# Expert weights loaded four tiles at a time, in runs of 32 KB, in a two-block transformer kernel

## The reference, cut to what matters

```python
def moe_expert_choice(h, router_w, w_gate, w_up, w_down):
    B_, T, _ = h.shape
    cap = CAPACITY_FACTOR * T // N_EXPERTS          # 32
    aff = jax.nn.softmax((h @ router_w).astype(jnp.float32), axis=-1)
    gate, idx = lax.top_k(jnp.swapaxes(aff, 1, 2), cap)
    xs = h[bidx, idx]
    hid = jax.nn.silu(jnp.einsum('becd,edf->becf', xs, w_gate)) * jnp.einsum('becd,edf->becf', xs, w_up)
    ye = jnp.einsum('becf,efd->becd', hid, w_down) * gate[..., None].astype(h.dtype)
    return jnp.zeros_like(h).at[bidx, idx].add(ye)
```

## Time and profile before

| | before |
|---|---|
| runs, median (lowest to highest) | 1550.55 us (1549.97 to 1551.77), 3 runs |
| profiled execution | 1551.3 us |
| its span, first to last instruction | 1549.5 us |
| TensorE busy | 1207.3 us, 78% of the span |
| VectorE, ScalarE busy | 562.5 us, 423.9 us |
| TensorE's granted clock, mean | 0.89 |
| moved by DMA | 520.9 MB, 336 GB/s over the span |
| packets of the SP queue | 118496 |

### The profile page before, as it was taken

One profiled execution on the slowest core, in us unless ns is written; L12 is line 12 of the kernel. 1 busy time (PEld: TensorE's weight loads), 2 busy tenths in 40 slices (PEclk: granted clock), 3 DMA queues, 4 the chain that ended last, 5 costly groups with the idle time before them and its releaser, 6 DMA issues.

```text
span 1549.5 us, 18615 instructions
## 1 busy us (share of the span) xinstructions
PE 1207.3 (78%) x8122; PEld 730.7 (47%) x8122; DVE 562.5 (36%) x829; ACT 423.9 (27%) x553; POOL 29.9 (2%) x36
## 2 busy tenths in 40 slices
PE   4999999999656656656666656656666899999998
PEld 1878899943111212111111111211211589999997
DVE  3887776511101101101101101101101497777566
ACT  2865646232000000000000000000000454467545
POOL 0012000000000000000000000000000000000000
PEclk9999999999778878778867888878778999999999
DMA  9546859699999999999999999999999855555551
GB/s 364 207 156 229 301 209 337 223 403 429 426 428 428 428 428 427 428 428 426 428 428 427 427 428 428 427 427 429 428 427 428 327 164 163 163 183 184 184 186 55
DMA packets 118719, 520.90 MB, mean 336 GB/s; under 512 B 7264, under 2 KB 85088, under 8 KB 90736
## 3 DMA queue, kind: packets, MB, share of 16 engines
q1 hardware_dynamic: 118496, 519.64, 83.9%
q10 hardware_dynamic: 144, 0.09, 0.0%
HBM read 518.66 MB, written 1.05 MB: 335 GB/s over the span
## 4 chain that ended last, share of the span: by engine, by line
DMA 53%; PE 43%; DVE 2%; ACT 1%; SPq 1%; issue 0%; DVEq 0%
DMA pair<-in_wu 27%; PE B L1697 16%; DMA pair<-in_wd 12%; DMA pair<-in_wg 11%; PE B L1705 6%; PE B L2113 4%; PE B L1709 3%; DMA wslot<-in_w_in 2%; PE B L1824 2%; PE B L2147 1%; PE B L1675 1%; PE B L1812 1%; PE B L1827 1%; DMA wslot<-in_w_out 1%; DMA wslot<-in_ada_w 1%; PE B L2074 0%
## 5 line engine op out<-in xcount | busy, mean ns | idle before, releaser
L2113 PE MATMUL B<-pair,xs 128*32 128x512 f32 x2048 | 323.1, 758 | 193.0 <-DMA pair<-in_wu 121.5
L2113 PEld LDWEIGHTS B<-pair,xs 128*32 128x32 f32 x2048 | 63.2, 124 | 413.0 <-issue 180.1
L2147 PE MATMUL B<-pair,hidT 128*32 128x512 f32 x1008 | 167.9, 799 | 102.1 <-DMA pair<-in_wd 96.6
L1697 PE MATMUL B<-hnh,whj 128*128 128x256 f32 x488 | 138.1, 283 | 0.0
L1697 PE MATMUL B<-hnh,wslot_r 128*128 128x256 f32 x488 | 137.6, 282 | 0.0
L1697 PE MATMUL B<-hn_r,whj 128*128 128x256 f32 x488 | 137.1, 281 | 0.0
L2147 PEld LDWEIGHTS B<-pair,hidT 128*32 128x32 f32 x1008 | 32.3, 128 | 218.6 <-DMA pair<-in_wd 143.2
L955 DVE TENSOR_TENSOR wslot_r<-wslot,whj 128x2048 fp32r<-128x2048 f32 x52 | 118.9, 2289 | 31.3 <-ACT whj L509 31.3
L509 ACT ACTIVATE whj<-wslot 128x2048 fp32r<-128x2048 f32 x51 | 97.2, 1913 | 87.6 <-PE B L1697 82.0
L1289 DVE SCALAR_TENSOR_TENSOR x<-B,mod,x 128x256 f32<-128x256 f32 x128 | 56.0, 480 | 163.5 <-PE B L2092 163.3
L1320 DVE COPY ye<-B 128x512 f32<-128x512 f32 x15 | 10.4, 692 | 269.6 <-PE B L2147 269.6
(11 more groups left out here) (505 smaller groups left out, 1908.8 us busy)
## 6 DMA issues: line engine op xcount, KB each, us to landing
pair<-in_wg SPq DMA_DIRECT2D x64, 2048.0 KB, 41.2
pair<-in_wu SPq DMA_DIRECT2D x64, 2048.0 KB, 40.9
pair<-in_wd SPq DMA_DIRECT2D x62, 2048.0 KB, 40.9
wslot<-in_w_in SPq DMA_DIRECT2D x58, 1024.0 KB, 5.2
aslot<-in_ada_w SPq DMA_DIRECT2D x20, 1024.0 KB, 7.2
wslot<-in_ada_w SPq DMA_DIRECT2D x4, 1024.0 KB, 9.1
wslot<-in_w_out SPq DMA_DIRECT2D x4, 1024.0 KB, 8.5
wslot<-in_wa SPq DMA_DIRECT2D x4, 1024.0 KB, 5.1
```

Of the source, the lines that this page charges most:

```text
L1697: mm = e.matmul(ps, w[:, k, :], x(k), start=k == 0 and j == 0, stop=k == kn - 1 and j == 2)
L2113: mm = e.matmul(B[b][32 * j:32 * j + 32, :], XS[x // 8][:, k, 32 * (x % 8):32 * (x % 8) + 32], tile_at_page(t)[:, 512 * j:512 * j + 512], ...
L2147: mm = e.matmul(B[3 + db][32 * r:32 * r + 32, :], hidT[:, 128 * c + 32 * j:128 * c + 32 * j + 32], v2(tile_at_page(t + c // 2))[:, c % 2, ...
```

## The change

The tiles stay as they are in size and number. From tile 28 on they are loaded in fours, 4 MiB to a transfer, in which each partition gets one contiguous run of 32 KB. The first 14 pairs stay pairs, in the places and behind the waits that they had, and so do the last two. There are four homes for the fours: the slots 0 to 3 and the pages 0 to 3, 4 to 7 and 8 to 11. The page pair 12 and 13 is no longer used for weights. A four waits until the last tile in any part of its home has been used.

So that a four is contiguous, gate and up tiles now hold the rows 512(k//4) + 4p + k%4, and down tiles eight rows to a partition. The gather reads H2k with a step of four, the product with the permuted identity becomes sixteen small products instead of four, and the moving operand of the gate and up products is no longer 512 numbers in a row but four of every eight, so that `hid` comes out in the order that the four transposes need. Three buffers of the second block change pages (one of WH2, c2), and some waits for a page to be free name other tiles.

```diff
-        WH2 = [put(f"whj{i}", 2048, page(p), FR) for i, p in enumerate((14, 15, 6))]
+        WH2 = [put(f"whj{i}", 2048, page(p), FR) for i, p in enumerate((14, 15, 0))]
...
-        c2, c2l = both("c2", 2048, page(0))
+        c2, c2l = both("c2", 2048, page(6))
...
-        TURN = [zpair(2), zpair(4), zpair(12), zpair(0), zpair(6), 0, 2, zpair(8), zpair(10)]
...
-        PAIRS = TURN[:2] + [EXTRA] + TURN[3:] + [APART] + 2 * (TURN[:2] + TURN[3:])
-        PAIRS += [TURN[i % 9] for i in range(12 * NE - len(PAIRS))]
...
+        LOADS = [(2 * i, 2, r) for i, r in enumerate((zone_at(2), zone_at(4), EXTRA, zone_at(0), zone_at(6), 0, 2, zone_at(8), zone_at(10), APART,
+                                                      zone_at(2), zone_at(4), zone_at(0), zone_at(6)))]
+        for t in range(28, 24 * NE, 4):
+            r = zone_at(8) if t == 24 * NE - 4 else (0, zone_at(8), zone_at(0), zone_at(4))[(t - 28) // 4 % 4]
+            LOADS += [(t, 2, r), (t + 2, 2, r + 2)] if t == 24 * NE - 4 else [(t, 4, r)]
...
+        def before(load):
+
+            t0, n, r = load
+            earlier = [x[0] + x[1] - 1 for x in LOADS if x[0] < t0 and any(in_slot(s, x) for s in range(r, r + n))]
+            return max(earlier) if earlier else None
+
+        def expert_src(t, n):
             e_, m, k = t // 24, t % 24 // 8, t % 8
             if m == 2:
-                return a["wd"][e_, 256 * k:256 * k + 512, :].rearrange("(p c) n -> p (c n)", c=4)
-            return a["wu" if m else "wg"][e_, 128 * k:128 * k + 256, :].rearrange("(p c) n -> p (c n)", c=2)
+                rows = a["wd"][e_, 1024 * (k // 4):1024 * (k // 4) + 1024, :].rearrange("(p c) n -> p (c n)", c=8)
+            else:
+                rows = a["wu" if m else "wg"][e_, 512 * (k // 4):512 * (k // 4) + 512, :].rearrange("(p c) n -> p (c n)", c=4)
+            return rows[:, k % 4 * SLOT:(k % 4 + n) * SLOT]
...
-                    e.wait_ge(*p_exp.at("tile", last_tile(zpair(10))))
+                    e.wait_ge(*p_exp.at("tile", last_tile(zone_at(11))))
                     e.dma_start(wgk[0:16, :], a["w_gk2"]).then_inc(*l_gk())
...
-            for b_ in range(2):
-                for hf in range(2):
-                    mm = e.matmul(B[4][64 * hf:64 * hf + 64, 0:16].rearrange("p (m q b) -> p b m q", m=2, b=2)[:, b_], ident[:, b_::2],
-                                  ffs.rearrange("p (m q h) -> p h m q", m=2, h=2)[:, hf], start=True, stop=True)
+            for b_ in range(4):
+                for hf in range(4):
+                    mm = e.matmul(B[4][32 * hf:32 * hf + 32, 0:16].rearrange("p (m q b) -> p b m q", m=2, b=4)[:, b_], ident[:, b_::4],
+                                  ffs.rearrange("p (m q h) -> p h m q", m=2, h=4)[:, hf], start=True, stop=True)
...
-                    mm = e.matmul(B[b][:, 0:32], H2k[:, i, 256 * (k // 2) + k % 2:256 * (k // 2) + 256:2], Pm[:, i, 0, :], start=i == 0, stop=i == 1)
+                    mm = e.matmul(B[b][:, 0:32], H2k[:, i, 512 * (k // 4) + k % 4:512 * (k // 4) + 512:4], Pm[:, i, 0, :], start=i == 0, stop=i == 1)
...
-                    if k % 2 == 0:
+                    if t == load_of[t][0]:
                         e.wait_ge(*landed[tile_page(t)].at("expert", t))
...
-                        mm = e.matmul(B[b][32 * j:32 * j + 32, :], XS[x // 8][:, k, 32 * (x % 8):32 * (x % 8) + 32], tile_at_page(t)[:, 512 * j:512 * j + 512], start=k == 0, stop=k == 7)
+                        mm = e.matmul(B[b][32 * j:32 * j + 32, :], XS[x // 8][:, k, 32 * (x % 8):32 * (x % 8) + 32], tile_at_page(t).rearrange("p (u q h c) -> p u h q c", u=2, h=2, c=4)[:, j // 2, j % 2], start=k == 0, stop=k == 7)
```

More of the change, by code:

```diff
@@ L298, in program @@
         ada_src = lambda q, k: a["ada_w"][k * 128:(k + 1) * 128, q * 2048:(q + 1) * 2048]
[L305 to L306 removed]
+        zone_at = lambda i: BASE + i
         EXTRA = BASE + MORE + AUX
         APART = EXTRA + 1
[L309 to L311 removed]
@@ L313, in program @@
+        load_of = {t: load for load in LOADS for t in range(load[0], load[0] + load[1])}
+        tile_page = lambda t: load_of[t][2]
+        homes = {(n, r): put(("pair" if n == 2 else "four") + str(r), n * SLOT, page(17) if r == EXTRA else slots_at + r * SLOT if r < BASE else page(r - BASE))
+                 for _, n, r in LOADS if r != APART}
         apart = (slots[4], put("apart", SLOT, page(15)))
         def tile_at_page(t):
-            return apart[t % 2] if tile_page(t) == APART else pairs[tile_page(t)][:, t % 2 * SLOT:t % 2 * SLOT + SLOT]
@@ L318, in program, with last_tile @@
[L318 to L325, removed]
+            t0, n, r = load_of[t]
+            return apart[t - t0] if r == APART else homes[n, r][:, (t - t0) * SLOT:(t - t0 + 1) * SLOT]
+        in_slot = lambda s, load: load[2] <= s < load[2] + load[1]
+        def last_tile(s):
+            return max(load[0] + load[1] - 1 for load in LOADS if in_slot(s, load))
@@ L461, in sync @@
                     experts(8)
-            for t in range(10, 24 * NE, 2):
+            for load in LOADS[5:]:
+                t = load[0]
                 if t == 10:
@@ L473, in sync @@
                     e.wait_ge(*p_proj.at("wo", 3))
[L474 to L477, removed]
+                elif before(load) is not None:
+                    e.wait_ge(*p_exp.at("tile", before(load)))
                 experts(t)
@@ L481, in sync @@
                 if n < SECOND + 4:
-                    e.wait_ge(*p_exp.at("tile", last_tile(tile_slot(n) // 2 * 2)))
+                    e.wait_ge(*p_exp.at("tile", last_tile(tile_slot(n))))
                 elif n == SECOND + 4:
-                    e.wait_ge(*p_exp.at("tile", max(i for i in range(24 * NE) if tile_page(i) == APART)))
+                    e.wait_ge(*p_exp.at("tile", last_tile(APART)))
                 else:
@@ L720, in scalar @@
                 if k == 7:
-                    e.wait_ge(*p_exp.at("tile", 2 * PAIRS.index(EXTRA) + 1))
+                    e.wait_ge(*p_exp.at("tile", last_tile(EXTRA)))
                     pp_left(0)
@@ L2144, in tensor @@
                     for i, part in enumerate(parts):
-                        e.wait_ge(*(l_last.at() if i < len(parts) - 1 else landed[tile_page(t)].at("expert", t + i)))
+                        if t + i == load_of[t][0] or len(parts) == 2:
+                            e.wait_ge(*(l_last.at() if i < len(parts) - 1 else landed[tile_page(t)].at("expert", t + i)))
                         for db, c, r in part:
```

18 lines of the change are left out of this document (9 added, 9 removed).

## The result

The changed kernel took 1559.38 us (median of 4 runs, 1556.91 to 1562.97), the kernel before 1551.12 us (4 runs, 1549.97 to 1551.77): a ratio of 1.0056, 95% interval 1.0032 to 1.008. It is slower by half a percent, where 1543.3 us and a gain were forecast. The profiled execution was the fastest of the four, 1556.91 us with a span of 1555.1 us, so the trace shows 5.6 us of the loss; the median has 8.3.

The account below looks back on a forecast made before the run. DMA loads of expert weights bound the second stage, to 1223 us, TensorE the stages around it. Packets -8.7, small products +0.4, gathers +0.2, end +0.8 sum to -7.3 us: 1543.3 us, range 1540.8 to 1550.8 for 8 in 10.

Parts of the forecast that it names:

- what is added ahead of the second stage: Extra TensorE work up to tile 7 delays the DMA-bound stage: 0.4 us for small products, 0.2 us for gathers.
- a queue that runs dry: DMA queue at the fours: first four covered by 3 us, later ones by fours issued behind; no gap, cost 0.
- The gathers: Ahead of tile 7, H2k loads at step four: 13 ns for each of 32, at most 0.4 us, 0.2 taken.
- the 2 us that the forecast named as a sign of being wrong: Start of the DMA stage: the prediction is wrong if tile 7 comes over 2 us late.
- what stands behind tile 7 has cover: Wider gathers after tile 7 cost nothing, as loads of tiles 24, 26 and the first fours are ahead.
- The packets: Expert weight loads: 144 fewer packets a four at 11 ns over 16 engines, 88 fours, 8.7 us saved.
- The 13.8 ns solved from the shares: Price of a DMA packet from packet counts and engine shares in two stretches; upper bound of 10.9 us saved.
- Rival 1: Expert loads: packets don't halve, or bytes bind the rate; no change, 1550.5 to 1552 us; chance 0.12.
- The small products at line 1918: Ahead of tile 7, sixteen products in place of four add 0.3 to 0.7 us; 0.4 taken.
- The end of the stage: After the last expert loads TensorE finishes later, delaying the second block by 0.4 to 1.8 us; 0.8 taken.
- a slow moving operand: Gate and up products slow with operands in fours; from 0.9 us a tile the gain is gone; chance 0.06.
- slow long runs: Expert loads: 32 KB runs read more slowly; 1% of rate gives 1552 us, 2% 1560.6; chance 0.08.

Follow-up runs that it names:

- e2: The kernel before, with only the load of tiles 18 and 19 made to wait for tile 5: 1561.21 us, ratio 1.0063.
- e7: The kernel before, with its two gathers reading H2k with a step of four instead of two: 1555.94 us, ratio 1.0035.
- e1: The changed kernel without the false wait of tiles 18 and 19 for tile 5: 1551.81 us, ratio 1.001 to the kernel before.
- e11: e6 with 512 numbers in a row as moving operand of the gate and up products: 1545.60 us, ratio 0.9961.
- e10: e6 with each four issued as two transfers of 2 MiB with runs of 16 KB: 1552.59 us.
- e12: e6 with each four as one transfer that gives each partition two runs of 16 KB: 1552.62 us.
- e5: e1 with H2k written so that the gather loads 128 numbers in a row: 1546.10 us, ratio 0.9976 to the kernel before.
- e6: e5 with tiles 376 to 379 loaded as two pairs: 1545.93 us, ratio 0.9967 to the kernel before.
- e4: e1 with each four cut into two transfers of 64 partitions each, runs of 32 KB: 2441.12 us, ratio 1.5702.

## Why the prediction was wrong, point by point

**The false wait: the step that failed.** The prediction rests on "the first 14 pairs stay pairs, in the places and behind the waits that they had". One of them didn't keep its wait. I had read the order of SyncE's rows and worked out the waits of the fours, but took the range test `in_slot` to be right for the two places that aren't pages. No term and no rival had it: in the sum, what is added ahead of the second stage has 0.4 and 0.2 us, and a queue that runs dry has "cost 0". With the late gathers it cost 12.2 us of DMA time in the changed kernel's trace; alone, in e2, it cost 10.5 us. The argument that it rests on was in the prediction, though: whatever holds back a load in that stretch moves the whole DMA stage.

**The gathers: a term of the sum that was mis-sized.** The forecast said "13 ns for each of 32 loads, 0.4 us at most", and took 0.2. It was 129 ns a load (325 against 196) and 3.5 us up to tile 7, of which 2.1 show in the time of tile 7, as the gathers started 1.4 us earlier. Even those 2.1 are over the 2 us that the forecast named as a sign of being wrong. I had taken the transposes of `hid` as the row for a step of four, 209 ns, and held it against 191 and 196 ns, which are loads of ordinary products. Transposes have a price of their own. In the window of the earlier trace rows the kernel before also has these two lines:

```profile
L2124 PEld LDWEIGHTS B<-ident,pr 128*128 128x128 f32 x4 | 0.4, 140 | 1.7 <-issue 1.7
L2052 PEld LDWEIGHTS B<-ident,af 16*128 16x128 f32 x2 | 0.2, 134 | 0.3 <-DVE af L1269 0.3
```

In the second the loaded operand is 16 x 128, which is the shape of the data `af`; its `ident` is 16 x 16. So a transpose loads its data, and that of the first, `pr`, is contiguous: 140 ns. Held against it, the step of four in `hid` cost 69 ns and not 13. That is still half of the 129, but as an estimate it gives 32 x 69 ns, some 2 us and not 0.2. The cost was 5.5 us in the medians of e7. I had also said that what stands behind tile 7 has cover. It had 3 us at tile 13, and with the slower gathers tile 13 came 4 us later in e1: its last hole.

The rule of the Trainium skill that I had set against it (Advanced Engine Details and Errata, Memory Cachelines) is that a new 16-byte line at each access pays. The traces agree: 190 ns contiguous, 196 at a step of two with two numbers to a line, 325 at a step of four with one, and the moving operand with four numbers in a row is free (e11).

**The packets: right in kind, somewhat large.** 105824 packets were counted, 105800 forecast; the rate went to 431 GB/s, 431 to 433 forecast. The 8.7 us were 6.6 by the rate in the trace and 5.7 to 7.0 by the medians of e10 and e12: 8 to 10 ns a packet instead of 11. The spans of e10 and e12 say more (8.8 and 9.7 us, 1.0 of it from the start of the gathers), so a price of 11 ns isn't ruled out. The 13.8 ns solved from the shares is above what the rate and the medians give. That the short transfers' own waits made it too large was argued and is not shown. Rival 1 didn't come.

**The small products at line 1918.** 32 records between 249.2 and 249.7 us, for 8 within 0.2: some 0.3 us, and 0.4 were taken.

**The queue and the end.** No four came late where the gathers were at their old speed (e5). The end of the stage was priced at 0.8 us. In the changed kernel ScalarE still waited 0.77 us for the second block's weights, so it was hidden there; where the other losses are gone it shows in the spans, 1.4 us between e5 and e6.

**The rivals.** Slower had a chance of 0.11, by a slow moving operand or slow long runs. Both were wrong; it came from a wait that the change wasn't meant to have. With that wait and the gather's step repaired, the forecast's mechanism gives 1546.10 and 1545.93 us (e5 and e6), 0.24% and 0.33% under the kernel before, so 4.3 and 4.5 us in the medians and not the 7.3 of the sum. That e6's profiled span is 1542.0, with 1542.2 forecast, is luck in part: its gathers start 1.2 us earlier than those of the kernel before.

**What stays open.** Kernels with the step of four spread over some 6 to 7 us (e1, e7, the changed kernel), those with a contiguous gather over 1 to 4, except for two of e5's ten runs. Their profiled executions were among the fastest, so the traces show less loss than the medians have. The time of the first gather moves by up to 2 us between the traces and carries the start of the DMA stage with it, but each kernel has one trace only, and why the slow gathers should widen the spread no run shows.

## What to carry to other kernels

When a change rewrites how waits are derived, list the waits of every load before and after and compare them, above all for the special places that don't follow the rule; a wait too many breaks nothing and shows only in the time. When a price is read off a row, hold it against a row of the same kind of instruction. Where a stage is bound by DMA, what lets its engines run dry at its start was lost one to one (e2), so price each operation ahead of the first loads that wait, and the layout of operands among them. Longer runs were worth their packets and no more: here some 6.7 us for 11136 of them, which the side effects of the layout that makes them possible easily eat up.

## What the runs showed of the hardware

- Stationary operands of 128 x 128 float32 load in 190 ns contiguous, 196 ns at a step of two and 325 ns at a step of four. Those of transposes load in 140 ns contiguous and 209 ns at a step of four. A moving operand of four numbers in every eight is as fast as a contiguous one (two tiles in 1.92 us in both).
- Doubling a run from 16 KB to 32 KB raised the rate from 428 to 431 GB/s; the number of transfers made no difference that could be measured (e10 and e12).
- Loads of 64 partitions each in runs of 32 KB, one behind the other, move 211 GB/s with all 16 engines busy (e4), half of the 431 GB/s of transfers of 128 partitions.
